# A one-core hybrid layer kernel: chunk-state steps issued by direction, loads queued ahead of stores, and the gate row summed by POOL

## The reference, cut to what matters

```python
def gmlp_mix(u, v, ln_g, ln_b, w_s, b_s):        # chunks of 128 tokens, 4 heads of 64
    u = gelu(u); vh = heads(gelu(v))
    vh = (vh - mean(vh)) * rsqrt(var(vh) + EPS) * ln_g + ln_b
    mixed = einsum('gpq,bnqgc->bnpgc', w_s, chunks(vh)) + b_s
    return u * mixed                              # then * silu(gm_g)

def wkv7_scan(r, w, k, v, a, b, s0, reverse):     # one direction, state S is 64 x 64 a head
    def step(S, inp):
        sa = S @ a_t
        S = S * w_t + outer(sa, b_t) + outer(v_t, k_t)
        return S, S @ r_t
# rwkv_branch: o = scan forward + scan backward over the latents, from the states that the
# context left; o = groupnorm(o) * g + b + bonus; then * silu(rw_g)

mod = silu(c) @ ada_w + ada_b                     # shift, scale, gate: 1024 columns each
x = x + gate * merge_branches([gm, na, rw, pl], ...)
```

## Time and profile before

| | |
|---|---|
| times of three runs | 2619.53, 2622.1 and 2624.96 us, median 2622.1 |
| profiled execution | 2618.64 us, of it the span 2616.9 us |
| busy: PE, PEld, DVE, ACT, POOL | 2262.2, 1857.7, 1531.4, 1020.9, 278.3 us |
| front stage | up to about 1270 us |
| recurrence, local half | about 1270 to 1844 us |
| recurrence, states | 1844.4 to 1913.3 us |
| recurrence, outputs | 1913.3 to 1980.1 us |
| attention, merge, output | from about 1983 us |

### The profile page before, as it was taken

How to read it: one execution, slowest core, us unless ns; L and a number is a source line. 1 busy time by engine, 2 the same in 40 slices (tenths; PEclk the granted TensorE clock), 3 DMA queues, 4 the chain that set the end, 5 groups by cost and what they waited for, 6 DMA issues and landing times. The chain is left out here.

```text
span 2616.9 us, 65618 instructions
## 1 busy us (share of the span) xinstructions
PE 2262.2 (86%) x26450; PEld 1857.7 (71%) x26450; DVE 1531.4 (59%) x2489; ACT 1020.9 (39%) x1754; POOL 278.3 (11%) x296
## 2 busy tenths in 40 slices
PE   4999999999899999999478877777664995898898
PEld 3788878888788878888366666666563673686687
DVE  5756665667655456666466666655542674776233
ACT  5444244445422134444245555544324664100321
POOL 0000000000000000000410001000232812000421
PEclk7999999999999999999699999999876997898999
DMA  6343323332433333332211111100757006676443
GB/s 225 114 126 117 120 93 113 112 108 93 133 92 99 98 106 107 108 116 96 66 38 38 38 38 48 54 24 24 238 198 230 18 2 202 240 265 221 164 144 120
DMA packets 263877, 300.11 MB, mean 115 GB/s; under 512 B 33274, under 2 KB 203386, under 8 KB 255482
## 3 DMA queue, kind: packets, MB, share of 16 engines
q1 hardware_dynamic: 261370, 288.65, 34.1%
q10 hardware_dynamic: 2304, 8.39, 0.8%
HBM read 194.62 MB, written 102.36 MB: 113 GB/s over the span
## 5 line engine op out<-in xcount | busy, mean ns | idle before, releaser
L715 PE MATMUL proj_ps<-h_hi,w_hi 128*128 128x512 f32 x1656 | 650.4, 393 | 29.1 <-DVE h_lo L465 20.9
L716 PE MATMUL proj_ps<-h_lo,w_hi 128*128 128x512 f32 x1656 | 647.3, 391 | 0.0
L717 PE MATMUL proj_ps<-h_hi,w_lo 128*128 128x512 f32 x1656 | 647.0, 391 | 0.0
L318 ACT CAST w_hi<-w_raw 128x512 fp32r<-128x512 f32 x420 | 255.2, 621 | 696.3 <-PE proj_ps L717 353.5
L715 PEld LDWEIGHTS proj_ps<-h_hi,w_hi 128*128 128x128 f32 x1656 | 312.5, 189 | 99.4 <-issue 27.9
L717 PEld LDWEIGHTS proj_ps<-h_hi,w_lo 128*128 128x128 f32 x1656 | 312.4, 189 | 65.9
L716 PEld LDWEIGHTS proj_ps<-h_lo,w_hi 128*128 128x128 f32 x1656 | 312.7, 189 | 63.5
L482 DVE TENSOR_TENSOR w_lo<-w_raw,w_hi 128x512 fp32r<-128x512 f32 x420 | 283.2, 689 | 44.5 <-ACT w_hi L318 43.8
L498 DVE TENSOR_TENSOR z_slots<-proj_ps,x_rows 128x512 f32<-128x512 f32 x174 | 120.2, 691 | 171.5 <-PE proj_ps L717 169.5
L967 POOL TENSOR_TENSOR neighbours<-z_halo 128x1792 f32<-128x1792 f32 x9 | 28.8, 3201 | 1270.4 <-DMA z_halo<-scratch_zT 1270.4
L498 DVE TENSOR_TENSOR x_rows<-proj_ps,x_rows 128x512 f32<-128x512 f32 x116 | 80.1, 691 | 109.5 <-PE proj_ps L717 103.5
(11 more groups left out here) (329 smaller groups left out, 3912.1 us busy)
## 6 DMA issues: line engine op xcount, KB each, us to landing
w_raw<-in_w_in SPq DMA_DIRECT2D x240, 256.0 KB, 3.0
scratch_gatesT<-z_slots SPq DMA_DIRECT2D x128, 256.0 KB, 2.7
m_gate<-scratch_gatesT SPq DMA_DIRECT2D x32, 1024.0 KB, 5.4
scratch_zT<-z_slots SPq DMA_DIRECT2D x108, 256.0 KB, 2.5
ada<-in_ada_w SPq DMA_DIRECT2D x4, 2048.0 KB, 15.4
mb_raw<-scratch_branchT SPq DMA_DIRECT2D x16, 512.0 KB, 5.4
scratch_mergedT<-m_y SPq DMA_DIRECT2D x8, 1024.0 KB, 5.7
y_raw<-scratch_mergedT SPq DMA_DIRECT2D x16, 512.0 KB, 4.8
```

The lines of the kernel that those rows point to most:

```text
L318: A.copy(wh[:, i, :, :], raw[:, q, :, :]).then_inc(w_hi, 1)
L715: T.matmul(out, wh[:, i, k, :], hi[:, o, k, :], start=(first and k == 0), stop=False, skip_group_check=not first)
L716: T.matmul(out, wh[:, i, k, :], lo[:, o, k, :], start=False, stop=False, skip_group_check=not first)
L717: last = T.matmul(out, wl[:, i, k, :], hi[:, o, k, :], start=False, stop=(k == 3), skip_group_check=not first)
```

## The change

In the local half, POOL now loads `ada_w` by its own queue, 512 KB at a time, multiplies each piece by its entry of silu(c) and adds it up in `chunk`-stage memory (`chain["gate"]`): two pieces behind `Z` in each of the units (0, 0), (0, 1), (8, 0) and (8, 1). The state half then only sums over partitions with 8 products of one column each (before the first block), and DVE adds the bias before the first block. The padded `rpbPad` is written during the local half too. `chain_step` takes a direction, and the gMLP pieces of PE and DVE stand between the two directions of a step in halves. The outputs use other PSUM banks, so that `outputs(0)` stands before the last `mixed`; `norm_dev` has three buffers; `load_g` and `load_y` of blocks 2 and 3 stand ahead of the first output block's store; `root_columns` and `finished` stand further back in their queues, and ACT has `squares(2)` and `squares(3)` earlier.

```diff
 # local half, SP
+            sp.wait_ge(pad_set, 1)
+            sp.dma_start(pad[:, GRID - 16:GRID + 15], t["na_rpb"].rearrange("l h r c -> (l h r) c")).then_inc(rpb_in, 16)
             load(1)
+            sp.wait_ge(rpb_in, 16)
+            src = pad[:].rearrange("r (a c) -> r a c", a=1).to_broadcast([4 * NDR, GRID, 2 * GRID - 1])
+            sp.dma_start(t["rpbPad"][:, :, 0:2 * GRID - 1], src).then_inc(pad_out, 16)
 # local half, POOL, at the end of unit(n, d)
+                if isinstance(n, int):
+                    k = (2 if n else 0) + d
+                    gate_rows(2 * k)
+                    gate_rows(2 * k + 1)
+            def gate_rows(k):
+                out = ada[:] if k else chain["gate"][:]
+                nc.gpsimd.dma_start(ada[:], t["ada_w"][0, k * P:(k + 1) * P, 2 * D:3 * D]).then_inc(ada_in, 16)
+                pool.wait_ge(ada_in, 16 * k + 16)
+                gate_sums.step(pool, nc.gpsimd.tensor_scalar(out, ada[:], s["mod"][:, 1, 2 * KT + k:2 * KT + k + 1], None, ALU.mult))
+                if k:
+                    gate_sums.step(pool, nc.gpsimd.tensor_tensor(chain["gate"][:], chain["gate"][:], ada[:], ALU.add))
 # state half, SP
-            load_ada(0)
             sp.dma_start(ada_bias[:], t["ada_b"].rearrange("l (m p) -> p (l m)", p=P)[:, 2 * KT:3 * KT]).then_inc(ada_b_in, 16)
...
-            load_ada(1)
...
             load_y(1)
             load_gates(1)
-            gm_v.after(sp, 3, "m")
+            load_g(2)
+            gm_v.after(sp, 3, "m1")
             store(0, 3, 3)
+            load_y(2)
+            load_g(3)
+            load_y(3)
             for b in range(NB):
-                if b + 2 < NB:
-                    load_g(b + 2)
-                    load_y(b + 2)
                 rw_v.after(sp, b, "out")
                 store(4, b, NB + b)
                 if b + 2 < NB:
                     load_gates(b + 2)
 # state half, PE
+            for m in range(KT):
+                last = T.matmul(ps[:, 4, m:m + 1], chain["gate"][:, m * P:(m + 1) * P], s["ones"][:, 0:1], start=True, stop=True)
+            last.then_inc(gate_ps, 1)
             for b in range(NB):
-                for k in range(EACH):
-                    chain_step(1 + AHEAD + b * EACH + k)
-                    if k < 2:
-                        turned_rows(b, k)
-                    elif k < 4 and b:
-                        mixed(b - 1, k - 2)
-                    elif k == 5 and b in (1, 3):
-                        gate(b // 2)
+                for j in range(2 * EACH):
+                    chain_step(1 + AHEAD + b * EACH + j // 2, j % 2)
+                    if j < 4:
+                        turned_rows(b, j)
+                    elif j < 8 and b:
+                        mixed(b - 1, (j - 4) // 2, j % 2)
 # state half, DVE
+            dve.wait_ge(ada_b_in, 16)
+            dve.wait_ge(gate_ps, 1)
+            V.tensor_tensor(s["mod"][:, 0, 2 * KT:3 * KT], ps[:, 4, 0:KT], ada_bias[:], ALU.add)
             for b in range(NB):
...
-                    if k in (3, 4) and b:
-                        scaled(b - 1, k - 3)
-                    if k == 5 and b:
-                        gated(b - 1)
-                    if k >= 6:
-                        normed(b, k - 6)
+                    if j in (8, 9) and b:
+                        scaled(b - 1, j - 8)
+                    if j in (10, 11) and b:
+                        gated(b - 1, j - 10)
+                    if j >= 14:
+                        normed(b, j - 14)
...
 # outputs, DVE (as on PE and ACT, the blocks' parts in another order)
             summed(1)
             statistics(0)
+            summed(2)
             statistics(1)
             finished(0)
-            summed(2)
+            summed(3)
+            statistics(2)
             finished(1)
-            statistics(2)
-            summed(3)
+            statistics(3)
             finished(2)
-            statistics(3)
             finished(3)
```

More of the change, by code:

```diff
@@ L1725, in _ @@
         def _(pe):
-            def chain_step(i):
-                for d in range(2):
-                    pe.wait_ge(s_done, 4 * (i - 1) + 2 * d + 2)
-                    for p in range(2):
-                        for h in range(2):
-                            last = T.matmul(ps[half(h), 6 + d, p * CH:(p + 1) * CH], chain["P"][half(h), d, chunk(d, i), p, :],
-                                            state(d, p, i)[half(h), :], start=True, stop=True)
-                    last.then_inc(p_done, 1)
@@ L1735, in turned_rows, with chain_step @@
[L1735 to L1748 removed]
+            def chain_step(i, d):
+                pe.wait_ge(s_done, 4 * (i - 1) + 2 * d + 2)
+                for p in range(2):
+                    for h in range(2):
+                        last = T.matmul(ps[half(h), 6 + d, p * CH:(p + 1) * CH], chain["P"][half(h), d, chunk(d, i), p, :],
+                                        state(d, p, i)[half(h), :], start=True, stop=True)
+                last.then_inc(p_done, 1)
@@ new lines, in turned_rows @@
+            def turned_rows(b, c):
+                r = c // 2
+                if c == 0:
+                    gm_in_a.after(pe, b, "v")
+                if c % 2 == 0:
+                    gm_n.earlier(pe, b, f"rows{r}")
+                for p in range(2):
+                    at = (c % 2) * BR + p * P
+                    last = T.matmul(ps[:, r, at:at + P], gin[:, b % 2, 2 + p, c * P:(c + 1) * P], chain["centre"][:], start=True, stop=True)
+                if c % 2:
+                    gm_p.done(last, f"rows{r}")
@@ L1749, in mixed @@
+            def mixed(b, p, part):
+                if part == 0:
+                    gm_n.after(pe, b, "rows1")
+                    gm_v.earlier(pe, b, f"s{p}")
+                for c in range(2 * part, 2 * part + 2):
                     for g in (2 * p, 2 * p + 1):
                         last = T.matmul(ps[half(g % 2), 2 + p, c * P:(c + 1) * P], rows[:, c, g * CH:(g + 1) * CH], wt[:, g, :], start=True, stop=True)
-                mix_p.done(last, f"mixed{p}")
-            def gate(n):
-                pe.wait_ge(ada_in, 16 * n + 16)
-                for k in range(4):
-                    for j in range(4):
-                        last = T.matmul(ps[32 * j:32 * j + 32, 4, 0:2 * P], gsc[:, 4 * n + k, :], ada[:, k, j * 2 * P:(j + 1) * 2 * P],
-                                        start=(n == 0 and k == 0), stop=True, skip_group_check=True)
-                last.then_inc(gate_ps, 1)
@@ L1761, in _ @@
-            chain_step(1)
+                if part:
+                    mix_p.done(last, f"mixed{p}")
+            chain_step(1, 0)
+            chain_step(1, 1)
             pe.wait_ge(w_in, 16)
@@ L1792, in outputs @@
                         rw_o.after(pe, b - 2, f"o{p}")
-                    elif b == 1:
-                        gm_v.after(pe, NB - 1, f"s{p}")
+                    elif b == 0:
+                        gm_n.after(pe, NB - 1, f"rows{p}")
                     for c in range(8):
```

165 lines of the change are left out of this document (67 added, 98 removed).

## The result

The changed kernel takes 2628.35 us (median of 20 runs) against 2622.82 us (median of 20) for the kernel before: ratio 1.0025, 95% interval 1.0014 to 1.0037. It is slower by 0.25%, where 2608.5 us was forecast. (Each ratio and interval here is from runs of the two kernels side by side; it isn't the quotient of the two medians, from which it differs by up to 0.0012.) Its profiled execution is the fastest of its 20, 2619.77 us, of it the span 2618.0 us; so its profile stands only 1.1 us above that of before.

| stretch | before | after | forecast |
|---|---|---|---|
| front stage | 1271.8 | 1270.7 | 0 |
| local half, unit (0, 1) | 29.3 | 33.2 | |
| whole local half | 572.6 | 576.1 | +2.5 |
| start of the states | 10.3 | 14.6 | +4.0 |
| four blocks of 8 steps | 58.3 | 71.1 | -2.3 |

What follows compares the result with a forecast made beforehand. Bounds seen: PE, then DVE, within state blocks; in the outputs PE's 13.03 us wait for g_in. Terms +4.0 - 2.3 + 0 - 16 + 2.5 = -11.8 us take 2618.64 to 2606.8, set at 2608.5; range 2599 to 2618.

Steps and rivals of the forecast that it cites:

- (c): State blocks: steps by direction with gMLP pieces in halves change order, not work; 0 us, bounds -5 and +2.
- (b): State blocks: gate products gone from the blocks; -2.3 us, bounds -3.6 and -1.9.
- Its own sign of being wrong: States: the prediction is wrong if block 2 changes by over 1 us at the same clock.
- the halves pay too: States: rival with the halves at -5 us and the bias load early at +1.5; 2601 us, chance 0.17.
- the slower rival: Local half: POOL's reading operations stop DVE on the path, 35 us in full; 2639 us, chance 0.05.
- (a): Start of the states: DVE must wait for gate products and the bias load; +4.0 us, bounds +1.5 and +8.
- (d): Outputs: PE's 13 us wait for g_in goes, gate loads bind the end; -16 us, bounds -19 and -10.
- (e): Local half: POOL's added operations hold DVE operations with two SBUF inputs; +2.5 us, bounds 0 and +8.
- POOL's operations cost more: Local half: rival with POOL's added work costing +8 us; 2614 us, chance 0.15.

Runs made afterwards that it cites:

- after_again: The changed kernel once more, unchanged, for a second profile: 2623.41 us, ratio 1.0022 to the kernel before.
- halves_only: The kernel before with nothing but the states' steps by direction, gMLP pieces in halves: 2631.9 us, ratio 1.0029.
- steps_whole: The changed kernel with whole state steps and whole gMLP pieces on PE and DVE, the rest as changed: 2619.72 us, ratio 0.9999.
- whole_late: The changed kernel with whole steps and DVE's bias wait and sum moved behind the last state step: 2615.82 us, ratio 0.9981.
- late_bias: The changed kernel with DVE's wait for the bias load and its sum moved behind the last state step: 2627.78 us, ratio 1.0023.
- outputs_only: The kernel before with only the outputs, loads, PSUM banks and third norm_dev buffer as changed: 2609.13 us, ratio 0.9950.
- outputs_again: outputs_only measured once more, as the base for outputs_rows and outputs_loads: 2604.73 us, ratio 0.9958.
- outputs_rows: outputs_only plus POOL's eight loads, scalings and seven sums in the local half, their result unused: 2611.03 us, ratio 0.9974.
- outputs_loads: outputs_rows with POOL only issuing the eight loads and waiting for them, no scalings or sums: 2614.71 us, ratio 0.9985.
- whole_late_norows: whole_late without POOL's eight loads, scalings and sums, leaving the gate row out of the computation: 2606.82 us, ratio 0.9939.
- whole_end: whole_late with the eight gate products moved behind outputs(1) and DVE's bias sum behind summed(1): 2611.82 us, ratio 0.9978.
- quarters: The changed kernel with half of a direction's gMLP products between its two pairs of state products on PE: 2646.97 us, ratio 1.0096.

## Why the prediction was wrong

**(c) is the step that failed.** It took the steps by direction at 0 us, bounds -5 and +2: "The halves change who stands where, not how much." The blocks took 71.1 us, where 58.3 less 2.3 for (b) were forecast: +15 us. (67.8 us and +12 in after_again.) The sentence ahead of it had PE full at 1.7 us a step in the first steps; with PE full, anything added to PE is on the path, and what is added is 0.15 to 0.245 us for each of 28 more changes, 4.5 to 6.3 us. The distances in the earlier trace rows are work and changes together; the prediction took them as work alone. Its own sign of being wrong came true: block 2 of halves_only is 1.08 us longer at the same clock. The rest goes with the clock: halves_only, mostly at a clock like before, lost 6.1 us in the blocks; the changed kernel lost 12.8 without gate products in them, with the clock back only 37 to 39 us behind the start of the states. Whole steps brought that to 17 to 19 us in both pairs of profiles (steps_whole, whole_late); which property of the halves holds the clock down is open. The rival "the halves pay too" had the wrong sign, and no rival had this case; the slower rival named another mechanism.

**(a) was right in size:** +4.2 us for +4.0, released by the bias load, which landed 7.2 us behind its issue (6.5 taken). What it missed is that the wait wasn't alone: late_bias took it away and won nothing, since the gate products are as late on PE (3.58 us; 3.41 taken) and the blocks behind them run at the lower clock level. Nothing in the prediction asked what a stall does to the clock of what follows.

**(b) was about half.** Block 1 with whole steps took 18.0, 17.7, 15.9, 17.8 and 15.4 us in the five kernels with gate products in it (before, outputs_only, outputs_again, outputs_rows, outputs_loads), and 15.7, 15.6, 14.9 and 16.1 in the four without (steps_whole, whole_late, whole_late_norows, whole_end): 1.3 us in the mean, with more scatter from the clock than that, for 2.3 taken. It is the one gain of the gate row's move, and smaller than its price.

**(d) was right:** 52.1 us from 67.1, -15.0 for -16, in the forecast's order: no wait for `g_in`, and the end bound by the gate loads of blocks 2 and 3 and by the spreading behind them (DVE idles 4.39 us before `finished(2)`, released by ACT's L1872).

**(e) was too small and had the wrong cause for most of it:** POOL's scaling takes 2.84 to 3.66 us, not 1.5. The added POOL work costs about 4 us (outputs_rows against outputs_again, 0.0016, not clear of zero) to 7 us (outputs_loads, 0.0027), in the range of 0 to +8; unit (0, 1) alone takes 4 us more. Of that, 0.2 to 0.8 us are the held scan, the cost that the prediction named. Some 3 us are PE's late instructions and the lower clock level behind them, which it didn't name, and they are there with the loads alone. The rival "POOL's operations cost more" had the sign right, but not the cause.

Put together with the measured terms: +4.2 (start) + 12.8 (blocks) - 15.0 (outputs) + 4 to 7 (local half) is +6 to +9 us, against a measured difference of 5.5 (0.0025). The blocks of after_again would give 3 less. So would the last row of the table, which this sum leaves out: behind the outputs the changed kernel takes 3.3 us less, where 0 was forecast. The kernels with the early write of `rpbPad` take 631.8 to 634.5 us there and the others 633.0 to 637.1; no run takes this apart. What remains is within the scatter of single profiles: the whole local half, which differs by units that the change doesn't touch, took 576 to 589 us in nine profiles with POOL's loads and 573 to 585 in five without (before, halves_only, outputs_only, outputs_again, whole_late_norows).

## What to carry to other kernels

Where an engine is full, finer interleaving isn't free: look at the distance between the starts of groups, and ask how much of it is the change from one shape of product to another. A stall ahead of dense work is priced by the clock of that work as well as by its own length. And when transfers are moved into a "free" stretch, look there for the engines' own instruction queue: an idle time that ends by "issue" in the middle of a group can be a sign that it is on the path.

## What the hardware showed that was not expected

- A change of PE between 64\*64 products and 128\*128 ones costs 0.245 us at the lower clock level and 0.17 at the upper, one between 64\*64 and 128\*64 about 0.20 and 0.15, with no wait added (quarters, steps_whole, halves_only, the changed kernel).
- In the blocks of quarters PE was busy for 79.44 of 87.43 us, and the granted clock was 0.50 throughout.
- PE starts again 2.2 to 2.4 us behind the start of a 16 KB packet of its instruction queue, which comes 1.5 to 2 us later beside a 512 KB load of POOL; in outputs_loads the granted clock was 0.50 for 3.4 us behind this stop.
- Beside POOL's 128x1024 scaling a DVE operation with a single tensor input (`log_w`, 128x512) takes 1.02 us instead of 0.42.
- Eight products of one column, with weights of 128x128, take 3.58 us at the lower level: as long as the state products of three steps (1.12 us each).
- Why the clock came back after 8.0 us in whole_late_norows, which still has these products (on zeros), and after 17.4 in whole_late, is open.
